# Two transformer-like blocks on one core: the memory's keys and values move into the second projection stage, weight splits move ahead of a store wait, and constants are waited for one by one

## The reference, cut to what matters

```python
h = rms_norm(x, norm_mix_g)                       # 512 tokens x 1024
(na_q, na_k, na_v, p_r, p_k, p_v, lat_w, lat_a, lat_g, mem_q,
 gate_na, gate_rw, gate_mem) = split_columns(h @ w_in)          # 5888 columns
y_na  = neighborhood_attention(na_q, na_k, na_v, na_rpb)        # 6 heads of 64
y_rw  = rwkv7_bidirectional(p_r, p_k, p_v, lat_w, lat_a, lat_g, ...)   # 6 heads, two directions
y_mem = memory_attention(mem_q, rms_norm(mem, norm_mem_g), w_mem_kv)   # mem: 256 tokens x 1024
merged = sigmoid(gate_na) * (y_na @ w_branch_na) + sigmoid(gate_rw) * (y_rw @ w_branch_rw) \
       + sigmoid(gate_mem) * (y_mem @ w_branch_mem)
x = x + merged @ w_out
x = x + expert_choice_ffn(rms_norm(x, norm_ffn_g), ...)         # 16 experts, 64 tokens each
return rms_norm(x, norm_final_g)

def memory_attention(q, mem_h, w_mem_kv):         # w_mem_kv: 1024 x 512
    mk, mv = jnp.split(mem_h @ w_mem_kv, 2, axis=-1)            # 256 x 256 each
    ...                                           # softmax(q mk^T / 8) mv, 4 heads
```

## Time and profile before

| | us |
|---|---|
| runs shown | 3312.02, 3317.74, 3319.58 |
| median | 3317.74 |
| the profiled execution | 3313.01 |
| its span, first to last instruction | 3310.9 |
| TensorE busy in it | 2830.3 |
| VectorE busy | 1266.3 |
| ScalarE busy | 789.4 |
| mean granted TensorE clock, of full | 0.907 |

### The profile page before, as it was taken

The page is one execution under the profiler, slowest core; times in us unless marked ns, Lnnn a source line. Parts: engine busy times, 40 slices in busy tenths (PEclk is TensorE's granted clock), DMA queues, the critical chain, the costliest instruction groups (busy, mean ns, idle before and its releaser), DMA issues. The chain is left out here.

```text
span 3310.9 us, 45205 instructions
## 1 busy us (share of the span) xinstructions
PE 2830.3 (85%) x18878; PEld 2035.8 (61%) x18878; DVE 1266.3 (38%) x2093; ACT 789.4 (24%) x1247; POOL 110.5 (3%) x90
## 2 busy tenths in 40 slices
PE   8999867699799698999598998667888888888887
PEld 7999745499799697777477886554323323233222
DVE  5664655443455533664243335523111111111112
ACT  3212154432333322441232332411000000000001
POOL 0000012000000000000002221000000000000000
PEclk9999977799899899999758999887999999899998
DMA  4336430344433453333300000656999999999994
GB/s 137 135 127 162 87 124 11 114 152 127 124 111 112 126 147 100 129 116 133 144 16 15 1 2 7 194 178 250 405 411 389 392 405 399 399 391 393 417 410 200
DMA packets 225397, 636.79 MB, mean 192 GB/s; under 512 B 39808, under 2 KB 137088, under 8 KB 200192
## 3 DMA queue, kind: packets, MB, share of 16 engines
q1 hardware_dynamic: 190096, 577.45, 46.6%
q10 hardware_dynamic: 35120, 56.74, 4.9%
HBM read 581.86 MB, written 49.92 MB: 191 GB/s over the span
## 5 line engine op out<-in xcount | busy, mean ns | idle before, releaser
L3293 PE MATMUL moe_bank<-moe_ring,moe_z 128*64 128x512 f32 x2048 | 525.1, 660 | 134.1 <-DMA moe_ring<-in_w_exp_up 133.3
L3293 PEld LDWEIGHTS moe_bank<-moe_ring,moe_z 128*64 128x64 f32 x2048 | 161.2, 150 | 439.1 <-issue 431.5
L3493 DVE TENSOR_TENSOR moe_sg<-moe_sg,moe_bank 64x512 f32<-64x512 f32 x64 | 44.1, 690 | 658.6 <-ACT moe_sg L3396 658.6
L64 PE MATMUL in_bank<-in_x_low,in_w_high 128*128 128x264 f32 x896 | 259.3, 289 | 6.1 <-DVE in_w_low L1194 6.0
L66 PE MATMUL in_bank<-in_x_high,in_w_high 128*128 128x264 f32 x896 | 255.6, 285 | 0.0
L65 PE MATMUL in_bank<-in_x_high,in_w_low 128*128 128x264 f32 x896 | 255.5, 285 | 0.0
L64 PE MATMUL merge_y<-merge_x_low,merge_w_high 128*128 128x264 f32 (+1 forms) x640 | 203.9, 319 | 56.4 <-DVE merge_w_low L533 50.4
L3321 PE MATMUL moe_bank<-moe_ring,moe_act_t 128*64 128x512 f32 x1024 | 230.6, 592 | 0.5 <-ACT moe_act_t L3403 0.5
L64 PE MATMUL up_prod<-up_x_low,up_w_high 128*128 128x264 f32 x704 | 201.7, 287 | 0.0
L66 PE MATMUL up_prod<-up_x_high,up_w_high 128*128 128x264 f32 x704 | 200.8, 285 | 0.0
L65 PE MATMUL merge_y<-merge_x_high,merge_w_low 128*128 128x264 f32 (+1 forms) x640 | 200.4, 313 | 0.0
(11 more groups left out here) (496 smaller groups left out, 5342.4 us busy)
## 6 DMA issues: line engine op xcount, KB each, us to landing
moe_ring<-in_w_exp_gate SPq DMA_DIRECT2D x64, 2048.0 KB, 13.5
moe_ring<-in_w_exp_up SPq DMA_DIRECT2D x64, 2048.0 KB, 17.9
moe_ring<-in_w_exp_down SPq DMA_DIRECT2D x64, 2048.0 KB, 9.0
in_w<-in_w_in SPq DMA_DIRECT2D x56, 512.0 KB, 3.4
front_w<-in_w_in SPq DMA_DIRECT2D x46, 512.0 KB, 3.4
up_w<-in_w_up SPq DMA_DIRECT2D x44, 512.0 KB, 5.0
p<-in_out ACTq DMA_DIRECT2D x48, 264.0 KB, 2.0
down_w<-in_w_down SPq DMA_DIRECT2D x8, 1408.0 KB, 9.0
```

The costliest lines, as they stand in the source:

```text
L64: nc.tensor.matmul(to, w_high, x_low, start=start, stop=False)
L3293: last = nc.tensor.matmul(bank[64 * g:64 * g + 64, s], xe[:, (e // BATCH) % 2, k, at:at + CAPACITY], ring[:, (3 * n + g) % RING, k * HALF: ...
L3493: nc.vector.tensor_tensor(sg[0:CAPACITY, s], sg[0:CAPACITY, s], bank[64:64 + CAPACITY, s], ALU.mult).then_inc(act_ready, 1)
```

## The change

Three things are changed.

**The stage `mem_kv` is gone, and `front` has four more tiles.** The host puts the columns of `w_mem_kv` behind those of `w_in`, so that the same weight loop runs over 50 tiles; tiles 46 to 49 multiply with the split memory (256 columns) in place of the tokens. After the load for tile 33 SyncE waits for `bonus_ready` at 2, since the memory is laid over the room of the preparation, then loads `mem` (1 MB) and its gain. ScalarE and VectorE get a `memory(i)` in step n = 33 + i: the split (i = 2, 3), squares and their sums (i = 4, 5, 6), and the root by Ln and Exp (i = 7). TensorE gets one product with `ones` after tile 39.

**ScalarE's step is reordered.** The store of a tile, with its wait for `out_ready`, moves from the end of step n to step n+1, behind the split of the next weights.

**In `rw` the constants have three semaphores.** TensorE starts with `ident`, VectorE with `masks`; the others are waited for where they are first used.

```diff
+FRONT_MEM = 33
+        mem = room[:, 0:KT * TM].rearrange("p (k t) -> p k t", k=KT)
+        mem_high = sb("mem_high", [P, KT, TM], F32R)     # shares memory with raw
             def _(sp):
-                for n in range(FRONT_TILES):
+                for n in range(tiles):                   # tiles = 46 + 4
                     if n >= 2:
                         sp.wait_ge(w_ready, n - 1)
                     sp.dma_start(w[:, n % 2] ..., w_dram[n * P:(n + 1) * P, :])
...
+                    if n == FRONT_MEM:
+                        sp.wait_ge(bonus_ready, 2)
+                        sp.dma_start(mem, mem_dram.rearrange("(k p) t -> p k t", p=P)).then_inc(mem_loaded, 16)
+                        sp.dma_start(mem_gain[:], mem_gain_dram).then_inc(mem_loaded, 16)
                 def products(n):                         # TensorE
                     pe.wait_ge(w_ready, n + 1)
                     if n >= 4:
                         pe.wait_ge(out_ready, n - 3)
+                    if n >= FRONT_TILES:
+                        pe.wait_ge(mem_low_ready, KT)
+                        for k in range(KT):
+                            done = three_passes(nc, bank[:, n % 4, 0:TM], w_high[:, s, k], w_low[:, s, k],
+                                                mem_high[:, k], mem_low[:, k], k == 0, k == KT - 1)
+                        done.then_inc(y_ready, 1)
+                        return
...
+                    if n == FRONT_MEM + 6:
+                        pe.wait_ge(mem_summed, 3)
+                        nc.tensor.matmul(bank[:, 7, 0:TM], ones[:], mem_sums[:, 0], start=True, stop=True)...
+                def memory(i):                           # ScalarE
+                    if i == 2:
+                        act.wait_ge(consts_ready, 6)
+                    if i in (2, 3):                      # after mem_loaded 32 and bonus_ready 2
+                        for k in range(4 * (i - 2), 4 * (i - 2) + 4):
+                            nc.scalar.activation(mem_high[:, k], mem[:, k], ACT.Copy, scale=mem_gain[:, k:k + 1])...
+                    if i in (4, 5):                      # i == 5 waits for mem_summed 1
+                        nc.scalar.activation(mem_sq, mem[:, 4 * (i - 4):4 * (i - 4) + 4], ACT.Square)...
+                    if i == 7:                           # after mem_sum_made 1
+                        nc.scalar.activation(mem_scale[:], bank[:, 7, 0:TM], ACT.Ln, bias=eps[:, 0:1], scale=1.0 / K)...
+                        nc.scalar.activation(mem_scale[:], mem_scale[:], ACT.Exp, scale=-0.5)...
-                for n in range(FRONT_TILES):             # ScalarE's loop
+                for n in range(tiles):
...
-                    elif 4 <= n < FRONT_TILES - 1:
+                    elif 4 <= n < tiles - 1:
                         split_w_high(n + 1)
+                    if n > RW_TILES:
+                        store(n - 1)                     # waits for out_ready n, then issues the store
                     for d, i in preparing(n):
                         prepare(d, i)
+                    memory(n - FRONT_MEM)
...
-                    if n >= RW_TILES:
-                        m = n - RW_TILES
-                        act.wait_ge(out_ready, n + 1)
-                        act.dma_start(p_dram[m * P:(m + 1) * P, :], out[:, m % 2]).then_inc(stored[m % 2], 16)
+                store(tiles - 1)
+                def memory(i):                           # VectorE
+                    if i in (2, 3):
+                        for k in range(4 * (i - 2), 4 * (i - 2) + 4):
+                            nc.vector.scalar_tensor_tensor(mem_low[:, k], mem[:, k], mem_gain[:, k:k + 1],
+                                                           mem_high[:, k].bitcast(F32), ALU.mult, ALU.subtract)...
+                    if i in (4, 5):
+                        nc.vector.tensor_reduce(mem_sums[:, i - 4], mem_sq.rearrange("p k t -> p t k"), X, ALU.add)...
+                    if i == 6:
+                        nc.vector.tensor_tensor(mem_sums[:, 0], mem_sums[:, 0], mem_sums[:, 1], ALU.add)...
+                nc.vector.memset(eps[:], EPS).then_inc(consts_ready, 1)
# finish(n), n >= 46: waits for mem_scale_ready 2, then bank[:, n % 4, 0:TM] * mem_scale
# rwkv7
-                for dst, src in ((ident, ident_dram), (masks, masks_dram), (member, member_dram), (eye2, eye2_dram),
-                                 (par, par_dram), (g2, g2_dram)):
+                sp.dma_start(ident[:], ident_dram).then_inc(ident_loaded, 16)
+                sp.dma_start(masks[:], masks_dram).then_inc(masks_loaded, 16)
+                for dst, src in ((member, member_dram), (eye2, eye2_dram), (par, par_dram), (g2, g2_dram)):
                     sp.dma_start(dst[:], src).then_inc(loaded, 16)
-                pool.wait_ge(loaded, 96)
+                pool.wait_ge(loaded, 64)
-                pe.wait_ge(loaded, 96)                   # before the first unit
+                pe.wait_ge(ident_loaded, 16)
-                dve.wait_ge(loaded, 96)
+                dve.wait_ge(masks_loaded, 16)
+                # loaded 64: VectorE in finish(0), TensorE before the gate product, ScalarE before the gate copy
# the chain of stages
-        project(nc, "mem_kv", d["mem"], d["w_mem_kv_2"], kv, gain_dram=d["norm_mem_g_2"])
```

More of the change, by code:

```diff
@@ L1902 @@
 MEM_WIDTH = MEM_HEADS * HEAD_DIM
+N_MEM = 256
 KEYS = 256
@@ L2189, with front @@
 FRONT_TILES = (3 * NA_WIDTH + 3 * RW_WIDTH + 2 * P + MEM_WIDTH + 3 * D_MODEL) // P
+MEM_TILES = 2 * MEM_WIDTH // P
 FRONT_PREP = (6, 19)
 FRONT_X = 4
-def front(nc, stage, h_dram, gains_dram, w_dram, par_dram, mu_l_dram, lora_dram, ar, bh, kh, v, bonus, ends, lat_g,
-          x_dram, p_dram):
+FRONT_MEM = 33
+def front(nc, stage, h_dram, mem_dram, gains_dram, mem_gain_dram, w_dram, par_dram, mu_l_dram, lora_dram, ar, bh, kh, v, bonus,
+          ends, lat_g, x_dram, p_dram, kv_dram):
     K, T = D_MODEL, SEQ
     N = RW_X * T
+    TM = N_MEM
+    tiles = FRONT_TILES + MEM_TILES
     with ExitStack() as ctx:
@@ L2234, in front @@
         mean = rate[:, 1]
+        mem = room[:, 0:KT * TM].rearrange("p (k t) -> p k t", k=KT)
+        mem_sq = room[:, KT * TM:KT * TM + KT * TM // 2].rearrange("p (k t) -> p k t", t=TM)
+        mem_sums = sb("mem_sums", [P, 2, TM])
+        mem_scale = sb("mem_scale", [P, TM])
+        mem_gain = sb("mem_gain", [P, KT])
+        with nc.sbuf_tensor(f"{stage}_raw", [P, 3, RW_X, T + 2], F32) as raw, nc.sbuf_tensor(f"{stage}_raw_l", [P, T + 2], F32) as raw_l:
+            pass
+        mem_high = sb("mem_high", [P, KT, TM], F32R)
+        mem_low = sb("mem_low", [P, KT, TM], F32R)
         bank = ps("bank", [P, 8, 512])
@@ L2288, in front @@
         bonus_ready = sem("bonus_ready")
+        mem_loaded = sem("mem_loaded")
+        mem_high_ready = sem("mem_high_ready")
+        mem_low_ready = sem("mem_low_ready")
+        mem_squared = sem("mem_squared")
+        mem_summed = sem("mem_summed")
+        mem_sum_made = sem("mem_sum_made")
+        mem_scale_ready = sem("mem_scale_ready")
         hv = h_dram.rearrange("(k p) t -> p k t", p=P)
@@ L2390, in _ @@
                         token_sums()
+                    if n == FRONT_MEM + 6:
+                        pe.wait_ge(mem_summed, 3)
+                        nc.tensor.matmul(bank[:, 7, 0:TM], ones[:], mem_sums[:, 0], start=True, stop=True).then_inc(mem_sum_made, 1)
                     for d, i in preparing(n):
@@ L2571, in finish @@
                             dve.wait_ge(stored[m % 2], 16 * (m // 2))
-                    nc.vector.tensor_tensor(to, bank[:, n % 4], scale[:], ALU.mult).then_inc(out_ready, 1)
+                    if n < FRONT_TILES:
+                        nc.vector.tensor_tensor(to, bank[:, n % 4], scale[:], ALU.mult).then_inc(out_ready, 1)
+                    else:
+                        dve.wait_ge(mem_scale_ready, 2)
+                        nc.vector.tensor_tensor(to[:, 0:TM], bank[:, n % 4, 0:TM], mem_scale[:], ALU.mult).then_inc(out_ready, 1)
                 def x_tiles(first):
@@ L2665, in _ @@
                 nc.vector.memset(blocks[64:P, 64:P], 1.0).then_inc(consts_ready, 1)
+                nc.vector.memset(eps[:], EPS).then_inc(consts_ready, 1)
                 nc.vector.memset(resets[:, 0:T:RCHUNK], 0.0).then_inc(consts_ready, 1)
-                dve.wait_ge(consts_ready, 5)
-                for n in range(FRONT_TILES):
+                dve.wait_ge(consts_ready, 6)
+                for n in range(tiles):
                     if n == 0:
@@ L2682, in _ @@
                             finish(m)
-                    elif n < FRONT_TILES - 1:
+                    elif n < tiles - 1:
                         split_w_low(n + 1)
@@ L2734, in rwkv7 @@
         loaded = sem("loaded")
+        ident_loaded = sem("ident_loaded")
+        masks_loaded = sem("masks_loaded")
         consts_ready = sem("consts_ready")
@@ L2855, in _ @@
                 act.wait_ge(gate_made, 1)
+                act.wait_ge(loaded, 64)
```

(9 more changed lines are left out.)

41 lines of the change are left out of this document (34 added, 7 removed).

## The result

The changed kernel took 3236.48, 3242.80, 3243.82 and 3248.12 us in four executions, median 3243.31; the kernel before took 3318.23 beside it (3312.02 to 3319.58, four). The ratio is 0.9776, with a 95% interval of 0.9755 to 0.9798: 75 us faster. The forecast was 3271, the range 3260 to 3287; the kernel is faster than the range allowed. The profiled execution took 3243.82, with a span of 3241.9, against 3313.01 and 3310.9 before: 69.0 us of the span to explain.

The account below looks back on a forecast made before the run. TensorE was taken to bound `front`, `att` (lower clock) and `rw` (upper), latency `mem_kv`. Terms -39.2 + 11.4 + 0.5 - 14.5 + 0.1 - 2.6 = -44.3 us gave 3268.7 or 3273.4, taken as 3271, range 3260 to 3287.

Parts of the forecast that it names:

- Parts 1 and 2: Removing `mem_kv` takes off 39.2 us whole; four tiles added to `front`, with one `ones` product, cost +11.4 us.
- the forecast's 5.8 us for that chain: `front`'s added tiles: loading, splitting and freeing a weight slot takes 5.8 us for two tiles, against 5.66 of products.
- Part 3: SyncE's new wait at tile 33 in `front` queues later loads behind it: +0.5 us, kept between 0 and 2.3.
- the reading of `mem_kv`'s loads: For SyncE's wait: 3 MB issued together landed in 10.0 us, so 1.5 MB take 5 and cost nothing.
- Part 4: ScalarE's split ahead of the store's wait in `front` removes TensorE's long waits and the clock falls behind them: -14.5 us.
- Part 5: `rw` starts when `ident` lands, 3.5 us after issue, instead of waiting for `g2`: -2.6 us, range 0 to -2.6.
- The step that failed: Rival that `att` runs at the upper clock: half way -18 us, giving 3253; chance 0.06, otherwise `att` unchanged.
- The forecast's own last sign of being wrong: The forecast is wrong if the clock's stretches in `att` and `rw` differ from before.
- VectorE kept up: Opposite of the rival that VectorE stays behind in `front`'s preparation, returning 14.5 us: 3285.5, chance 0.10.
- the last tiles did not starve: Opposite of the rival that slow weight loads starve `front`'s four last tiles at 4.2 us each: 3279, chance 0.08.
- `rw` had the upper clock: Opposite of the rival that `rw` runs at the lower clock, 10.5 us more per unit, up to 3524; chance 0.02.

Follow-up runs that it names:

- experiment 3: Kernel before with only ScalarE's reordering in `front` (store's wait behind the next split): median 3300.75, ratio 0.9932.
- experiment 4: Kernel after with ScalarE's reordering undone, the store again at the end of its step: median 3281.72, ratio 0.9878.
- experiment 9: Kernel after with the six constants of `rw` on one semaphore again, waited for all together: median 3247.77, ratio 0.9799.
- experiment 11: Kernel after with eight extra products of ones ahead of tile 46's products, so `att` starts 3.5 us later: median 3247.07, ratio 0.9785.
- experiment 8: Kernel after with products of ones on TensorE through its pauses around `att` and at `rw`'s start: median 3228.02, ratio 0.9750.
- Experiment 2: Kernel before with an Exp as last activation of `mem_kv`, taking the table load out of `att`: median 3311.05, ratio 0.9986.
- experiments 1 and 7: Kernel after with a Sqrt ending `front`, putting the table load back (median 3254.64); with a 1280-column ScalarE copy before `att`'s first exponential instead (median 3266.18).
- experiment 6: Kernel before with three 512-column products of ones filling TensorE's pause before `att`'s first turn, table load kept: median 3281.06, ratio 0.9899.

## Why the forecast missed, point by point

**Parts 1 and 2, the stage and the four tiles: right.** -41.7 was forecast from `front`'s first product to `att`'s first load, with all of parts 1 to 4; it was -42.4. Tiles 46 to 49 took 2.83, 2.83, 3.06 and about 2.9 us (forecast 2.8 to 3.0), the one product with `ones` some 0.45. The 0.1 to 0.2 us that the weights' two slots might cost were 0.2 (tile 48); the forecast's 5.8 us for that chain is 3.4 + 2.3 = 5.7 by its own terms. The splits, squares and sums of the memory cost no wait of TensorE, as assumed. The two tables for Ln and Exp on ScalarE did fit into step 40:

```profile
1545.27 1.28 ACT L2469 ACT_TABLE_LOAD   x1
1546.57 0.47 ACT L2469 ACTIVATE front_mem_scale<-front_bank,front_eps 128x256 f32<-128x256 f32 x1
1547.06 1.28 ACT L2472 ACT_TABLE_LOAD   x1
1548.35 0.42 ACT L2472 ACTIVATE front_mem_scale<-front_mem_scale 128x256 f32<-128x256 f32 x1
```

The last line, an Exp, is the one that takes the table load out of `att`, and its effect one stage on was not looked for.

**Part 3, SyncE's wait: the mechanism right, the size between two readings.** 0.5 forecast, 0.9 measured (tiles 33 and 34 took 6.13 and 5.61 us, 0.69 and 0.17 over 5.44). The chain is the one described: tile 34's weights, issued at 1501.52, 2.0 us into tile 32, came 7.2 us later, behind the memory's 1 MB; ScalarE waited for them, and TensorE for the split. The 0.5 stood between two ways of adding the loads up: landed 6 us behind tile 32's start and free, or 10.7 behind it and 2.3 us late. They landed 9.2 behind it, so the reading of `mem_kv`'s loads that the forecast leaned on was 3.2 us short:

```profile
1500.16 0.38 SPq L2345 DMA_DIRECT2D front_room<-in_mem  x1
...
1508.77 1.05 ACT L2439 CAST front_w_high<-front_w 128x1024 fp32r<-128x1024 f32 x1 [7.91 <-DMA front_w<-in_w_in]
...
1511.13 0.50 PE L64 MATMUL front_bank<-front_x_low,front_w_high 128*128 128x512 f32 x1 [0.53 <-DVE front_w_low L2595]
```

**Part 4, the reordering: right.** -14.5 forecast; -15.0 in experiment 3 and 15.7 in 4. From tile 3 on TensorE has one wait above 0.1 us, the 0.53 above, and the clock is at 1.00 from tile 1 to the end. The stretches of part 4 came out as added up: tile 15's start to tile 18's 18.95 us (forecast 18.96), tile 27's to tile 31's 24.40 (24.40). Tile 16 took 7.62 us and tile 17 5.89, together 2.63 over two plain tiles: three bonus products of 0.88.

**Part 5, `rw`'s constants: right in the mechanism, -4.2 instead of -2.6.** `ident`'s landing was taken from the earlier trace rows as 3.5 us; it was 1.8 after, and 1.7 with the old semaphore in experiment 9, so the 3.5 was that execution's, not the kernel's. TensorE's first transpose came 5.3 to 6.1 us behind `ident`'s issue in the six profiles with the old waits, and 1.7 to 1.9 in six of the eight with the new (3.3 in experiment 11's, where `ident` landed late, and 3.1 in experiment 8's, with two products ahead of it). By the medians of experiment 9 it is 4.5 or 7.9 us, by which set of the kernel after is taken; between its profile and the kernel after's, TensorE's first transpose differs by 3.5.

**The step that failed** is the one by which `att` keeps its time and stands in the sum with nothing: "the rows speak against it", chance 0.06, at half the price, -18. The reason given, that TensorE is busy throughout `att` and the clock stayed down all the same, took the state of the clock for a property of the work. The forecast's own last sign of being wrong, stretches of the clock in `att` that differ from before, came. Experiment 2's kernel shows otherwise: its profiled execution runs the same 368 matmuls mostly at the upper clock in 76.79 us, and eight of its ten executions are some 22 to 33 us longer at a lower mean clock. `att` took 29.9 us less, which together with the forecast's own terms is the whole miss: -44.3 was forecast for the sum, the terms of it measured -42.4 - 4.2 = -46.6, and with -29.9 it is -76.5, before the spread of the other stages. Where the forecast lay, at 3271, are the low executions of experiments 1 and 7, at 3261.3 to 3274.6.

Two readings of the trace before pointed at it. The clock was up for 6.80 us in `att` before it fell (1650.00, above), which the earlier trace rows, whose stretch begins at 1657, left out: this stage could be at either level. And the table load of 1.28 us at 1653.72 stands in the middle of the pause behind which it fell; an edit that changes the last activation of the stage before takes it away. Both can be read before the change is run. They would not have given the odds: experiment 2 takes that load out and stays low in eight of ten.

The other rivals did not come: VectorE kept up (tiles 5.44 us apart), the last tiles did not starve, `rw` had the upper clock in all its units but the first.

## What to carry to other kernels

A stage that is all TensorE at the lower clock isn't given: look at what TensorE did in the few us ahead of the fall, and price the other level at its full worth. Count a table load of ScalarE, and any gap that a change makes or closes, at the start of the next stage too; a few products of ones in such a gap made `att` 27 us shorter in the kernel before. Where executions of one kernel fall in two groups, compare within a group and count the groups: a median of ten can hide an edit that only moves the odds.

## What the runs showed that was not expected

- The lower clock holds through work that leaves TensorE hardly a gap: 75.00 us at 0.50 with TensorE busy 74.41 (experiment 4). The same work stays at 1.00 with it busy 39.45 of 44.00 us (kernel after).
- Filling a pause of 2.77 us took `att` from 105.27 to 78.28 us in the kernel before (experiment 6: 3281.06 at a ratio of 0.9899).
- Two functions, Ln and Exp, one directly after the other, each had a table load of 1.28 us (1545.27 and 1547.06). The Trainium skill ("ScalarE: Activation LUTs", "Table sets: the hidden batching unit") lists a set that holds both functions, one load instead of two. The trace doesn't agree, and the measurement decides.
- `ident`'s 64 KB landed 1.7 to 1.8 us behind their issue in ten of fourteen profiled executions and 3.2 to 3.5 us in four, under the old semaphore (both values, three times each) as under the new (once 3.2, in experiment 11). One landing time, read from one execution, was off by a factor of two.
